# Half of the input projection's chunks computed inside the stick-breaking stage (hybrid stick-breaking, gated linear and PEER layer, Trainium2)

## What is computed

```python
mod = (silu(c) @ w_ada + b_ada)                       # 6 x 1024: shift, scale, gate, twice
h = rms(x) * (1 + scale1) + shift1
proj = h @ w_in      # sb_q, sb_k, sb_v, g_q, g_k, g_v, g_lr, g_r
sb_out = head_rms(stick_breaking(sb_q, sb_k, sb_v))   # 8 heads x 64
log_a = log_sigmoid(g_lr @ w_gate_up + b_gate) / 16
gla_out = head_rms(gla_chunked(g_q, g_k, g_v, log_a)) * silu(g_r)   # 4 heads
x = x + gate1 * (concat(sb_out, gla_out) @ w_out)
# then rms, modulation, PEER retrieval over 128^2 experts, gated add, final rms
```

## Time and profile before

| | us |
|---|---|
| three executions | 1627.75, 1629.53, 1625.63 |
| median | 1627.75 |
| profiled execution, span from first to last instruction | 1622.9 |
| profiled execution, its own time | not given beside its span |
| TensorE, VectorE, ScalarE, GpSimd busy in the span | 1557.8, 1290.2, 712.4, 387.6 |

### The profile page before, as it was taken

How to read it: one execution, slowest core, us unless ns; L and a number is a source line. 1 busy time by engine, 2 the same in 40 slices (tenths; PEclk the granted TensorE clock), 3 DMA queues, 4 the chain that set the end, 5 groups by cost and what they waited for, 6 DMA issues and landing times.

```text
span 1622.9 us, 23639 instructions
## 1 busy us (share of the span) xinstructions
PE 1557.8 (96%) x8161; PEld 1371.0 (84%) x8161; DVE 1290.2 (79%) x2612; ACT 712.4 (44%) x1123; POOL 387.6 (24%) x328
## 2 busy tenths in 40 slices
PE   6999997979999999999999999999999999999997
PEld 4787665669899999999999999998888888888886
DVE  6764474549598999999999999757888888888887
ACT  4323473444334333434477677634333333333333
POOL 0000000412433233323122222122333333333310
PEclk9999989999999999999999999999999999999999
DMA  8763300016778877888789899899999999999982
GB/s 339 267 248 113 124 1 1 26 36 206 271 256 247 285 271 262 271 258 279 260 307 318 315 323 319 318 326 342 344 351 359 353 355 349 362 346 365 346 298 102
DMA packets 176963, 426.83 MB, mean 263 GB/s; under 512 B 15168, under 2 KB 99280, under 8 KB 172112
## 3 DMA queue, kind: packets, MB, share of 16 engines
q1 hardware_dynamic: 139984, 291.14, 51.2%
q0 software_dynamic: 36864, 134.23, 23.8%
HBM read 372.88 MB, written 52.43 MB: 262 GB/s over the span
## 4 chain that ended last, share of the span: by engine, by line
PE 72%; DMA 1%; DVE 1%; ACT 0%; issue 0%; DVEq 0%; ACTq 0%
PE ps_y L1924 11%; PE ps_y L1928 11%; PE ps_y L1926 11%; PE ps_u L1132 10%; PE ps_u L1134 10%; PE ps_u L1133 10%; PE ps_g L1627 5%; PE ps_q L1314 1%; PE ps_q L1316 1%; PE ps_q L1315 1%; DMA activations<-u_act 1%; PE ps_s L1326 1%; PE ps_u L1959 0%; DVE y_scaled L1870 0%; DVE row L1891 0%
## 5 line engine op out<-in xcount | busy, mean ns | idle before, releaser
L1132 PE MATMUL ps_u<-h_hi,u_hi 128*128 128x384 f32 x1024 | 348.9, 341 | 2.6 <-DVE u_lo L1122 2.0
L1134 PE MATMUL ps_u<-h_hi,u_lo 128*128 128x384 f32 x1024 | 344.9, 337 | 0.0
L1133 PE MATMUL ps_u<-h_lo,u_hi 128*128 128x384 f32 x1024 | 344.8, 337 | 0.0
L1795 ACT CAST v_hi<-v_raw 128x1024 fp32r<-128x1024 f32 x128 | 134.7, 1052 | 326.1 <-issue 315.6
L1191 POOL DMA_INDIRECT row<-in_v,row_index x128 | 172.6, 1348 | 377.0 <-DVE h_row L1211 316.9
L1191 POOL DMA_INDIRECT row<-in_u_rows,row_index x128 | 150.4, 1175 | 448.4 <-DVE row_dots L1198 377.9
L1853 DVE TENSOR_TENSOR v_lo<-v_raw,v_hi 128x1024 fp32r<-128x1024 f32 x128 | 160.4, 1253 | 101.0 <-ACT v_hi L1795 101.0
L1924 PE MATMUL ps_y<-v_hi,w_hi 128*128 128x512 f32 x768 | 238.0, 390 | 0.3 <-DVE w_lo L1840 0.3
L1926 PE MATMUL ps_y<-v_lo,w_hi 128*128 128x512 f32 x768 | 237.0, 389 | 0.0
L1928 PE MATMUL ps_y<-v_hi,w_lo 128*128 128x512 f32 x768 | 237.0, 389 | 0.0
L1122 DVE TENSOR_TENSOR u_lo<-u_raw,u_hi 128x1024 fp32r<-128x1024 f32 x128 | 166.9, 1310 | 75.1 <-ACT u_hi L1115 75.0
(11 more groups left out here) (295 smaller groups left out, 2306.5 us busy)
## 6 DMA issues: line engine op xcount, KB each, us to landing
u_raw<-in_u SPq DMA_DIRECT2D x128, 512.0 KB
v_raw<-in_v SPq DMA_DIRECT2D x128, 512.0 KB
w_ada<-in_w_ada SPq DMA_DIRECT2D x24, 1024.0 KB, 7.1
activations<-u_act SPq DMA_DIRECT2D x128, 192.0 KB
gate_tiles<-g_tile SPq DMA_DIRECT2D x12, 2048.0 KB
gates<-gate_tiles SPq DMA_DIRECT2D x32, 768.0 KB
act<-activations SPq DMA_DIRECT2D x128, 192.0 KB
w_proj<-in_w_proj SPq DMA_DIRECT2D x16, 512.0 KB, 4.0
```

The lines of the kernel that those rows point to most:

```text
L1132: pe.matmul(out, self.hi[n][:, k], hi, start=(k == 0), stop=False)
L1133: pe.matmul(out, self.hi[n][:, k], lo, start=False, stop=False)
L1134: last = pe.matmul(out, self.lo[n][:, k], hi, start=False, stop=(k == KD - 1))
```

## The change

It splits the 16 chunks: 0 to 7 stay in the front stage, 8 to 15 (`GLQ`, `GLK`, `GLR`) are computed in stick-breaking, half a chunk (12 matmuls) behind each step's scores. They have one PSUM bank, so the outputs of a head pair have one and not two. ScalarE copies a finished chunk at the end of every odd step and then makes the high part of the chunk two further on; GpSimd makes the low parts of chunks 8 to 15, the first two of them in the front stage. The front stage has three turns after its first two chunks; a turn takes three halves of the modulation (low, half, half, low, half on VectorE), and seven halves stand behind the low parts of values 4 to 10. Its Fori loops are written out. SP loads chunks 10 to 15 in stick-breaking, behind the semaphore clears, and `w_out` at the start of gated linear. Silu moves from the front stage to gated linear, between the squares and the first Ln, followed by a load of the table for Exp and Ln. In memory, `h` keeps its space, the ring of softplus becomes one tile per step of a pair, three gated linear operands are made in place of others, and gated linear's output goes where `SBQ` was. The rest of the diff follows from these (names, signatures, `mixer_back` reading from the new place).

```diff
+FRONT_PROJ = GLQ
...
+class Projections:
...
+    PAIR = 2
...
+    def load(self, sp, c):
+        n = c % self.PAIR
+        if c >= self.PAIR:
+            sp.wait_ge(self.lo_done, c - self.PAIR + 1)
+        sp.dma_start(self.raw[n][:], self.io["w_proj"][c]).then_inc(self.w_in[n], 16)
+
+    def high(self, act, c):
+        n = c % self.PAIR
+        act.wait_ge(self.w_in[n], 16 * (c // self.PAIR + 1))
+        if c >= self.PAIR:
+            act.wait_ge(self.prod, c - self.PAIR + 1)
+            act.wait_ge(self.lo_done, c - self.PAIR + 1)
+        act.copy(self.hi[n][:], self.raw[n][:]).then_inc(self.hi_done, 1)
+
+    def low(self, eng, c):
+        n = c % self.PAIR
+        eng.wait_ge(self.hi_done, c + 1)
+        if c >= self.PAIR:
+            eng.wait_ge(self.prod, c - self.PAIR + 1)
+        eng.tensor_tensor(self.lo[n][:], self.raw[n][:], self.hi[n][:].bitcast(F32), ALU.subtract).then_inc(self.lo_done, 1)
+
+    def products(self, pe, c, out, h_hi, h_lo, rows):
+        n = c % self.PAIR
+        for k in rows:
+            pe.matmul(out, self.hi[n][:, k], h_hi[:, k], start=(k == 0), stop=False)
+            pe.matmul(out, self.hi[n][:, k], h_lo[:, k], start=False, stop=False)
+            last = pe.matmul(out, self.lo[n][:, k], h_hi[:, k], start=False, stop=(k == KD - 1))
+        if KD - 1 in rows:
+            last.then_inc(self.prod, 1)
+
+
+def front_stage(nc, io, keep, t16, v8, gx, proj):
...
+        N_ADA, EARLY, TURNS, PAIR = 6 * D // COLS, 2 * D // COLS, FRONT_PROJ // 2, proj.PAIR
...
+        LATE = [(m, half) for m in range(EARLY, N_ADA) for half in range(2)]
+        PER_TURN = 3
+        BY_TURN = [LATE[j * PER_TURN:(j + 1) * PER_TURN] for j in range(TURNS - 1)]
+        BY_VALUE = {HALF + n: late for n, late in enumerate(LATE[PER_TURN * (TURNS - 1):])}
+        COLUMNS_AFTER_TURN = [[m for m, half in late if half == 1] for late in BY_TURN]
+        COLUMNS_AFTER_VALUE = {v + 1: m for v, (m, half) in BY_VALUE.items() if half == 1}
...
+            for j in range(TURNS - 1):
+                for m, half in BY_TURN[j]:
+                    load_ada(m, half)
                 for n in range(PAIR):
-                    load_w(2 * i + e + 1, n)
...
+                    proj.load(sp, (j + 1) * PAIR + n)
             for v in range(HALF, N_VAL):
                 load_values(v)
+                if v in BY_VALUE:
+                    load_ada(*BY_VALUE[v])
+                if v == KD:
+                    for n in range(PAIR):
+                        proj.load(sp, FRONT_PROJ + n)
...
+            for n in range(PAIR):
+                proj.low(pool, FRONT_PROJ + n)
...
+            for c in range(FRONT_PROJ - PAIR):
+                proj.high(act, c + PAIR)
+                keep_chunk(c)
...
-            act.wait_ge(kept, N_PROJ)
-            act.activation(t16[:, GLR:GLR + 4], t16[:, GLR:GLR + 4], ACT.Silu)
...
+                if KD < v <= KD + PAIR:
+                    proj.high(act, FRONT_PROJ + v - KD - 1)
...
+            for j in range(TURNS - 1):
                 for n in range(PAIR):
-                    low(2 * i + e + 1, n)
-                    sum_rows(m, n, 2 * e + n, i + 3, e)
...
-            projection_turns(dve, turn)
-            for half in range(2):
-                sum_rows(N_ADA - 1, half, 2 + half, TURNS // 2 + 2, 1)
+                    proj.low(dve, (j + 1) * PAIR + n)
+                    for m, half in BY_TURN[j][n * 2:n * 2 + 2]:
+                        sum_rows(m, half)
...
                 values_low(v)
+                if v in BY_VALUE:
+                    sum_rows(*BY_VALUE[v])
                 if v == KD:
                     keep_values(dve, 0)
-                if v == KD + 2:
-
-                    dve.wait_ge(kept, N_PROJ)
+                if v == KD + 4:
...
+                    dve.wait_ge(kept, FRONT_PROJ)
...
-        self.q_in = sb("q_intra", [P, GLA_PAIRS, T])
-        self.q_st = sb("q_state", [P, GLA_PAIRS, T])
...
-        self.k_in = sb("k_intra", [P, GLA_PAIRS, T])
+        self.q_in, self.q_st, self.k_in = self.mag, self.bc, self.k_mid
...
         elif n == 5:
-            act.activation(self.q_st[:], self.bc[:], ACT.Exp, scale=1.0 / GLA_TAU).then_inc(self.exps, 1)
+            last_row = self.bc[:].rearrange("p a (c t) -> p a c t", c=N_CHUNKS)[:, :, :, GLA_CHUNK - 1]
+            act.activation(self.carry[:], last_row, ACT.Exp, scale=1.0 / GLA_TAU).then_inc(self.exps, 1)
         elif n == 6:
             act.activation(self.k_dec[:], self.k_dec[:], ACT.Exp, scale=1.0 / GLA_TAU).then_inc(self.exps, 1)
         elif n == 7:
-            last_row = self.bc[:].rearrange("p a (c t) -> p a c t", c=N_CHUNKS)[:, :, :, GLA_CHUNK - 1]
-            act.activation(self.carry[:], last_row, ACT.Exp, scale=1.0 / GLA_TAU).then_inc(self.exps, 1)
+            act.wait_ge(self.exps, 3)
+            act.activation(self.q_st[:], self.bc[:], ACT.Exp, scale=1.0 / GLA_TAU).then_inc(self.exps, 1)
...
             dve.wait_ge(self.exps, 5)
+            dve.wait_ge(self.kept, GLR)
             k, q = self.t16[:, GLK + p], self.t16[:, GLQ + p]
...
-        ND, IN_FLIGHT, RING, LAG = SB_HEADS // 2 * TB, TB, 3, 2
+        ND, IN_FLIGHT, LAG = SB_HEADS // 2 * TB, TB, 2
+        BESIDE = N_PROJ - FRONT_PROJ
...
-        soft = sb("softplus", [P, RING, 2, T])
+        soft = [sb(f"softplus{s}", [P, 2, width(s)]) for s in range(TB)]
...
-        ps_o = [pb(f"ps_o{n}", [P, T]) for n in range(2)]
+        ps_o, ps_f = pb("ps_o", [P, T]), pb("ps_proj_beside", [P, T])
...
-            sp.dma_start(keep["w_out"][:], io["w_out"]).then_inc(keep["w_out_in"], 16)
             for done in keep["spent"]:
                 sp.sem_clear(done)
+            for c in range(FRONT_PROJ + proj.PAIR, N_PROJ):
+                proj.load(sp, c)
...
-                if p >= 2:
-                    pe.wait_ge(o_kept, p - 1)
+                if p >= 1:
+                    pe.wait_ge(o_kept, p)
...
+            def beside(d):
+
+                c, half = FRONT_PROJ + d // 2, d % 2
+                if half == 0:
+                    pe.wait_ge(proj.lo_done, c + 1)
+                    pe.wait_ge(proj.kept, c)
+                proj.products(pe, c, ps_f[:], keep["h_hi"], keep["h_lo"], range(half * KD // 2, (half + 1) * KD // 2))
...
             for d in range(ND + LAG + 1):
                 if d < ND:
                     scores(d)
+                if d < 2 * BESIDE:
+                    beside(d)
                 if LAG <= d < ND + LAG:
                     suffix(d - LAG)
...
-                    x = soft[:, d % RING, :, 0:width(s)]
+                    x = soft[s][:]
                     act.wait_ge(z_done, d + 1)
-                    if d >= RING:
-                        act.wait_ge(lo_done, d - RING + 1)
+                    if d >= TB:
+                        act.wait_ge(lo_done, d - TB + 1)
...
+                if d % 2 == 1 and d // 2 < BESIDE:
+                    c = FRONT_PROJ + d // 2
+                    act.wait_ge(proj.prod, c + 1)
+                    act.copy(t16[:, c], ps_f[:]).then_inc(proj.kept, 1)
+                    if c + proj.PAIR < N_PROJ:
+                        proj.high(act, c + proj.PAIR)
...
         @block.gpsimd
         def _(pool):
             operands.constants(pool)
-
...
+            for c in range(FRONT_PROJ + proj.PAIR, N_PROJ):
+                proj.low(pool, c)
...
+        def _(sp):
+            sp.dma_start(keep["w_out"][:], io["w_out"]).then_inc(keep["w_out_in"], 16)
+
         @block.gpsimd
         def _(pool):
...
         def _(act):
             for c in range(TB):
                 act.activation(sq[:, c], catT[:, c], ACT.Square).then_inc(sq_done, 1)
+            act.activation(t16[:, GLR:GLR + 4], t16[:, GLR:GLR + 4], ACT.Silu)
+            act.preload_act_table_set("natural_log_exp_and_others")
...
-                dve.tensor_copy(catT[:, TB + h], ps_o[h][:])
+                dve.tensor_copy(t16[:, SBQ + h], ps_o[h][:])
...
-                for n in ("h_hi", "h_lo"):
-                    keep[n] = front.enter_context(nc.sbuf_tensor(f"{n}_mixer", [P, KD, T], F32R))
-                front_stage(nc, io, keep, t16, v8, gx)
-
-            keep["w_out"] = msb("w_out_raw", [P, KD, KD, P])
-            catT = msb("catT", [P, KD, T])
-            with ExitStack() as linear:
-                operands = LinearOperands(nc, linear, t16, gx)
-                stick_breaking(nc, io, keep, t16, v8, catT, operands)
-                gated_linear(nc, keep, v8, catT, operands)
             for n in ("h_hi", "h_lo"):
                 keep[n] = sb(n, [P, KD, T], F32R)
+            t16, v8, gx = msb("t16", [P, N_PROJ, T]), msb("v8", [P, 2, TB, T]), msb("gate_x", [P, GLA_PAIRS, T])
+            with ExitStack() as weights:
+                proj = Projections(nc, weights, io)
+                front_stage(nc, io, keep, t16, v8, gx, proj)
+                catT = msb("catT", [P, TB, T])
+                linear = mix.enter_context(ExitStack())
```

(45 more changed lines are left out.)

144 lines of the change are left out of this document (61 added, 83 removed).

## The result

Seven executions of the changed kernel took 1630.38 to 1633.37 us, median 1631.9; seven of the kernel before, beside them, had a median of 1627.3. The ratio is 1.0035 (95% interval 1.0023 to 1.0047): **0.35% slower**, 4.6 us. The profiled execution took 1631.9 us for a span of 1630.2, so 1.7 us lie around a span; on that footing the profiled one of before (1622.9) was a little faster than its median. Of the 7.3 us between the two spans I explain those up to the first query product of the retrieval, 7.0 us; behind it the stretches of unchanged code vary by some 4 us either way between the profiles shown here, so that stage starts tell more than spans. Stage starts have a spread too: experiments 1, 7 and 9 leave the front stage as it is in the changed kernel, and in their profiles stick-breaking starts at 156.4, 157.2 and 156.4 us, not 157.6.

The account below looks back on a forecast made before the run. TensorE was taken to bound the front stage, while stick-breaking had TensorE time to spare. Front stage -33.1, stick-breaking +30.6 and gated linear +3.5 summed to +1.0 us: 1628.8, say 1629, range 1621 to 1638.

Parts of the forecast that it names:

- the slower one: Case of a slower kernel, chance 0.35: mainly rival 2, with 0.03 for halves that fail to fill stick-breaking's gaps (1641 us).
- the forecast one of no change: Whole kernel: nearly a wash, 1624.5 to 1631 us; chance 0.40.
- Front stage: Projections: 43.5 us of matmul removed, but VectorE's order and late loads leave 33.1 us saved, ends 29 and 38.
- TensorE leaves the turns at 100.7: Front stage's turns: TensorE loses 5.8 us to late low parts, by product 1.9, 0.5, 2.0 and 1.4.
- I take 3 for both: Front stage, ahead of values(8): two GpSimd lows hold up VectorE by 3 us together, up to 2.2 each.
- Rival 2: Clock falls at copy waits, values(8)'s bank wait and behind Silu: +8 us, 1637; chance 0.35, with a front stage saving only 30.
- Stick-breaking: Chunks added beside the scores: 85.4 + 4.1 + 14.0 + 1.5 = 105.0 us against 74.4, 30.6 us more, ends 28 and 37.
- the four steps that I named: Stick-breaking steps 4, 6, 10 and 14: half a chunk waits for ScalarE's copy, 1.1, 0.65, 1.7 and 0.65 us, 4.1 in all.
- the slow start of 1.5: Start of stick-breaking: the clock falls at the hand-over as before, 0 to 2.5 us, taken as 1.5.
- Gated linear: Silu and two table loads ahead of the first Ln delay the third head sum: 3.5 us more, ends 3 and 6.
- that chance of 0.1: Gated linear: each table switch costs the skill's 2.66 us, making the price 6.3 and the time 1631.6; chance 0.1.
- Rival 1: Faster: the front stage keeps up, 38 us saved, and stick-breaking's clock never falls, +29; 1622 us, chance 0.25.

Follow-up runs that it names:

- experiment 1: Changed kernel with Silu moved from gated linear to the end of stick-breaking, behind ScalarE's last step; ratio to the kernel before 1.0007, median 1626.26 us.
- experiment 7: Changed kernel with one product pass of three for the chunks in stick-breaking, 8 matmuls a chunk in place of 24; one execution, 1617.2 us.
- experiment 9: Changed kernel with ScalarE copying a finished chunk ahead of the weights and operand steps, not behind them; ratio to before 1.0011, median 1627.01 us.
- experiment 6: Changed kernel with the edits of experiments 1, 2, 3 and 5 together; ratio to before 0.9956, median 1617.86 us.
- experiment 3: Changed kernel with SP issuing the first w_proj chunk ahead of the third w_ada half in each turn; ratio to before 1.0026, median 1629.7 us.
- experiment 2: Changed kernel with the high parts of chunks 8 and 9, and so GpSimd's two lows, four values later; ratio to before 1.0025, median 1629.81 us.
- experiment 5: Changed kernel with VectorE's order in the turns low, half, low, half, half; ratio to before 1.0049, median 1633.43 us.
- Experiment 4: Changed kernel with ten chunks in the front stage and six in stick-breaking, in place of eight and eight; ratio to before 1.0047, median 1633.45 us.
- experiment 10: Changed kernel with the edits of experiments 1, 3, 5 and 9, and both highs of chunks 8 and 9 behind the last value; ratio to before 0.9919, median 1610.32 us.

## Why the prediction was right or wrong

The predicted time, 1629.0, was 2.9 us under the measured median and the range held it; of the cases the slower one came true (chance 0.35), and not the forecast one of no change (0.40). That the total is so near is in part luck: by stages the sum missed by 6.0 us (+7.0 for +1.0), while the medians differ by 4.6. The prediction also put some 5 us around a span, where 1.7 are measured.

**Front stage: the term that was mis-sized**, -27.3 for -33.1. The steps hold in kind, but lose more than their terms say:

- "TensorE leaves the turns at 100.7": it left at 104.2. The four waits for low parts in the turns are 1.77, 0.67, 1.79 and 1.79 us for 1.9, 0.5, 2.0 and 1.4, 6.0 and not 5.8, with the low of product 4 at 72.47 and its wait for `w_proj` as argued. Product 6 lost nothing, as I said, though its low was late (87.42, `w_proj` 6 landing 12 us after ScalarE was ready for it). From start to start each wait costs some 0.3 us more than the idle that is shown, since the last matmul ahead of it is recorded with 0.39 us and the first one behind it takes 0.34 to the next, for 0.2265 in a row: 1.3 us more than 5.8 in all. The rest is clock, which I charged with nothing here: the granted clock was 0.79 from 96 to 104 us, which cost 1.7 us, and 0.58 from 48 to 56 us, in code that hardly differs from before, so that product 2 started at 58.99 and not at 58.45.
- "I take 3 for both" lows' lock-out: the half took 3.9 us longer. values(8) started at 130.87 and not at 126, of which 4.0 us are TensorE's late arrival (124.7 and not 120.7), handed on by the gate product, the gate activations and the low of value 8, and 0.9 the lock-out.
- Behind it came the clock again: 0.50 and 0.67 in the two windows shown, some 1.8 us; the wait of 0.9 that I had for half (11,1) didn't come.

So the 5.8 us are 0.5 at the start, 1.3 of waits in the turns, 1.7 of clock, 0.5 up to values(8), 0.9 of lock-out and 1.8 of clock, less the 0.9. About 3.5 are slow clock. Rival 2 had named one place of it, "the bank wait of values(8)"; the end of the turns it hadn't. And that part isn't fixed to the change: with the same front stage, experiments 1 and 9 were granted 1.00 from 96 to 104 us, and experiment 7 0.79; from 48 to 56 us experiment 6 was granted 1.00, where experiment 3, with the same order of loads, was granted 0.57.

**Stick-breaking: right**, +30.6 for +30.6, in this profile; the stage took 104.9 us in experiment 1, with Silu at its end, and 106.5 in 2, 3 and 5, which leave its code alone. The copy waits are at the four steps that I named, 1.02, 0.62, 1.68 and 0.62 us for 1.1, 0.65, 1.7 and 0.65. Two parts hide errors that cancel: the slow start of 1.5 wasn't there, and small gaps between the steps, with the last suffix's wait of 1.23, made up for it. Experiment 7 limits what my sum means. It added matmuls as if TensorE bounded every step at full clock; with two thirds of the added ones gone only 44% of their time came back, since longer waits and a lower clock (0.91) took the rest. Experiment 4 shows the same with a quarter gone. The sum holds at this size, with TensorE busy for 97 of 105 us; it wouldn't have for a smaller one. Nor are 4 us of copy waits a fixed price: experiment 9 removed them by the order of two steps. The six GpSimd lows cost nothing, as argued: no suffix waits for softplus but the last.

**Gated linear:** +5.3 for +3.5. The hole is the 3.65 us of the argument. What was missing is the clock behind it, low from 270 to 276 (0.72), 1.7 us; that was rival 2's third place. ScalarE, with its two table loads:

```profile
264.78 1.28 ACT L838 ACT_TABLE_LOAD   x1
266.07 1.91 ACT L838 ACTIVATE t<-t 128x2048 f32<-128x2048 f32 x1
267.99 1.28 ACT L839 ACT_TABLE_LOAD   x1
269.28 1.27 ACT L843 ACTIVATE rstd_sb<-ps_upd,eps 128x512 f32<-128x512 f32 x2
```

Each load takes 1.28 us and the next operation starts 0.01 us later. The Trainium skill (ScalarE: Activation LUTs, What ACT_TABLE_LOAD costs) gives 2.66 with its drain; the trace doesn't agree, and that chance of 0.1 fell.

**The mixer's back**, which I had at nothing, gained 1.6: before had a clock of 0.72 from 298 to 304 us, and the same work of after (306 to 312) 1.00. The stage took 62.4 us in all the experiments but the first, which took 64.0 as before did, so this too is clock and not the change. w_out's late load cost nothing that shows.

**Rival 2's points.** Its bank wait and its Silu hole were followed by a low clock, its copy waits, up to 1.68 us, weren't: the whole of stick-breaking was granted 1.00. The price of the slow clock was some 5 us in all (1.7 at the turns' end, 1.8 and 1.7), not 8, and part of it came back in the mixer's back. The Trainium skill (TensorE: Matmul & The Clock Gate, What's actually happening) has activity as what releases the throttle; stick-breaking, with TensorE busy for 97 of 105 us, agrees. **Rival 1** was right of the clock in stick-breaking and wrong of the front.

**The signs.** Held: stick-breaking 105 us long, TensorE busy for over 90% of it at 1.00, four copy waits, the hole beneath Silu, and `w_out` landed (at 275.4) before its first reader (290.5). Not held: stick-breaking started at 157.6, behind the 147 to 155 that I gave, and VectorE had gaps of about 3 us, two in the turns (3.24 and 3.18) and two among the values (2.90 and 3.10); the ones in the turns are of the late `w_proj`, as experiment 3 shows.

**On the whole**, what makes this change slower isn't the split but its orders: with the same split, experiment 10 turns +0.35% into -0.8%. Against the rival that the clock alone is the loss: experiments 1, 2 and 9 each removed the wait they were aimed at (3.2, 3.9 and 3.9 us of it), experiment 3 at least 1.3 us of its own, and experiments 6 and 10, with several edits at once, kept the gain. But experiments 1, 2 and 3 moved the first query product by 4.6, 1.0 and 0.4 us, and in 2 and 3 low clock in stick-breaking took part of what was won. Why the clock falls at one place and not at another isn't settled: the falls moved from kernel to kernel, even where the code up to them is the same, and no run here isolates their cause.

## What to carry to other kernels

When work is moved out of a stage that one engine fills, walk the orders of the other engines through at once: here the stage lost 43.5 us of matmul and only 27.3 us of time, because loads, VectorE's sums and GpSimd's lows were still placed for the longer stage. A queue's order (a small load behind a large one that waits for its slot, a bank-freeing copy behind an engine's own chain) costs a wait at each turn, and changing it can be free; fix such orders together, since one alone (experiment 5) can find the next limit at once. And judge each step by stage starts in the trace, not by the total, which moves by as much as the effects do; but look first how far a stage moves that the edit leaves alone, 1.2 us for the front stage and 1.5 us for stick-breaking here.

## What the runs showed of the hardware that was not expected

- With 3.9 us less of one wait in experiment 2, the clock fell to 0.58 in a stretch of stick-breaking that had 1.00 in the changed kernel. It lies just behind the first copy wait, which is as long in both (1.02 us). Stick-breaking was 1.5 us longer in experiments 3, 5 and 6 too:

```profile
174.00:178.00 4.00, 4.00 (x12) 3.11 (x12) 2.54 (x5) 1.72 (x4) 2.37 (x1) 0.58 0.00 0
```

- The clock also fell where TensorE was busy for 7.77 of 8.00 us (96 to 104 us of after, 0.79), after turns whose waits were 1.8 us at most, and it didn't in stick-breaking, with waits as long. In experiments 1 and 9, whose code is the same up to there, the clock stayed at 1.00 in that stretch.
- Two GpSimd lows in a row held a chain of four multiply-adds on VectorE for 3.9 us more than its 3.11, two thirds of the lows' 5.58 us; I had taken 3. Two of the four took the whole delay: they ran for 2.73 and 2.71 us where the one ahead took 0.75, and each ended 0.5 us behind a low (127.14 behind 126.59, 129.88 behind 129.34), as the one of the earlier trace rows did. The Trainium skill (SBUF — State Buffer, SBUF: two separate sides) has the pair as an exclusive lock, held for a whole instruction; these ends and the 3.11 of experiment 2 agree.
